# A decoder layer's attention: when norm factors and operand splits are computed, and how rotary scores are multiplied

## The chip, the core and the metric

One Trainium2 chip, of which the kernel uses one core. A core has TensorE (PE, matrix products; PEld its weight loads), VectorE (DVE), ScalarE (ACT), GpSimd (POOL) and SyncE (SP, which here issues most transfers), and they run side by side, held together by semaphores only. The metric is the device time of one execution in microseconds. The kernel before takes 1430.42 us, the median of three runs (1427.04 to 1432.64).

## The reference

A decoder layer over 1024 tokens of width 1024: adaLN-modulated RMS norm, one input projection, eight heads of stick-breaking attention (width 64) and four heads of softmax attention (MLA), an output projection, and a SwiGLU FFN. What the change touches is this:

```
q = rms_norm(q, q_norm); k_nope = rms_norm(k_nope, ...); k_rope = rms_norm(k_rope, ...)
q = concat([q[..., :128], apply_rope(q[..., 128:], positions)])          # 4 heads, 128 + 64 wide
k = concat([k_nope, broadcast(apply_rope(k_rope, positions), 4 heads)])  # one rotary key for all heads
o_mla = causal_softmax_attention(q, k, v_mla)                            # scores of 192 products each
mixed = concat([rms_norm(o_sb, out_norm_sb), rms_norm(o_mla, out_norm_mla)])
x = x + gate1 * (mixed @ w_out)
```

## The kernel before, in words

Matrix products are taken in a rounded fp32 type. To keep fp32 precision each operand x is split into a high part H (ScalarE's rounding copy) and a low part L = x - H (VectorE's subtraction), and a product is the sum of three: H.H + H.L + L.H (`three`, L1579). A *split* here is such a pair of instructions on a [128, 1024] tile; they count semaphores m_h and m_l.

The softmax attention runs in 32 units: two pairs of heads p (0, 1), two heads e in each, eight query blocks of 128 in each head, in the order ORDER0, so that the units of a head have 1, 7, 3, 5, 6, 4, 8 and 2 key blocks. v is the unit's number in its pair (0 to 15), u = 16 p + v. The sequence positions are reversed, hence the causal part lies to the right. TensorE's order is written out by hand (L1921): in turn n it issues `scores(n+2)`, `turned(n)` (transposes of the weights, 128 columns each) and `values(n-1)`. `scores` takes segments of up to 512 columns: three products for the 128 plain rows, three for the rotary rows (`mla_scores`, L1764), and a mask on the first segment. The rotary rows of both heads of a pair lie in one tile QRK[:, p] (64 rows each), and the head is picked by the key's tile: KRH[e] and KRL[e] have the rotary key in 64 rows and zeros, written by GpSimd, in the other 64.

VectorE, per unit (`mla_step`, L1260): maximum of the scores, its negation, its share of the copy of the turned weights of u-2, the finish of u-3. ScalarE, per unit (L790): exponential with row sum, its share of that copy (pmT). Both then do splits: at v = 2 q and k of the pair's second head; at v = 12 rotary part, q and k of the next pair's first head (p = 0), or q and k of the first stick-breaking pair (p = 1). `mla_ready` (L1833) makes TensorE wait for the counts of m_l.

The stick-breaking attention has 64 units, in four pairs of heads (i = 0 to 3), 16 units each, numbered v. ScalarE makes two sigmoids, omb and beta, VectorE a scan (left) and a product, then come turns and values as above. Its scores take two products for a segment and not three: the high part and the low part of a head's 64 rows of q are stacked in one 128-row tile headQ, against the key's high part twice, headKH, and its low part with zeros, headKL. SP builds these tiles by five transfers for each head (`stack_head`, L388).

In the last pair ScalarE also makes the norm of the softmax outputs: the squares' sums of o_mla for eight token blocks at v = 0 to 7 (`mla_squares`), VectorE the mean at v = 9, GpSimd the power -0.5 (nrs), and ScalarE scales the blocks at v = 10 to 13, two in each, after waiting for nrs at v = 10. Each of these stands at the head of ScalarE's step, ahead of omb. The blocks are then transposed, rounded and multiplied by w_out, whose first two splits stand at v = 11 and 12.

Of the kernel before, what the change touches and what calls it, by code (L numbers as in the profile page):

```python
# [23 lines left out]
P = 128  # L24
# [80 lines left out]

SPLIT1, SPLIT0 = 2, 12
SB_Q, SB_K, SB_OUT = 4, 6, 11
# [12 lines left out]
def build(nc, xT, cols_d, rows_d, pos_d, ada1_d, ada2_d, win_d, qup_d, kvup_d, wout_d, gu_d, down_d, x2_d, t_d, out_d):  # L120
# [82 lines left out]
    pmT = [at(f"pmT{s}", [P, S], F32, 18 + 4 * s) for s in range(2)]  # L203
    KRH = [at("KRH0", [P, S], F32R, 26), at("KRH1", [P, S], F32R, 98)]
    KRL = [at("KRL0", [P, S], F32R, 30), at("KRL1", [P, S], F32R, 102)]
# [4 lines left out]

    mrH = [at("mrH0", [P, S], F32R, 138), at("mrH1", [P, S], F32R, 142)]
    mrL = [at("mrL0", [P, S], F32R, 202), at("mrL1", [P, S], F32R, 158)]
# [77 lines left out]
    t_out = [ctx.enter_context(nc.semaphore(f"t_out{k}")) for k in range(2)]  # L290
    traw_in = [ctx.enter_context(nc.semaphore(f"traw_in{k}")) for k in range(2)]
    head_in = [ctx.enter_context(nc.semaphore(f"head_in{e}")) for e in range(2)]
    raw_in = [ctx.enter_context(nc.semaphore(f"raw_in{k}")) for k in range(2)]
# [3 lines left out]
    def after(n):  # L297

        return n + 1 + PRIME
# [56 lines left out]
    def _(sp):  # L356
# [31 lines left out]
        def stack_head(p, e):  # L388

            own, other = slice(64 * e, 64 * e + 64), slice(64 - 64 * e, 128 - 64 * e)  # L390
            sp.wait_ge(sem["s_h"], 2 * p + 2)
            sp.wait_ge(sem["s_l"], 2 * p + 2)
            for dst, src in ((headQ[e][own, :], pairQH[own, :]), (headQ[e][other, :], pairQL[own, :]), (headKH[e][own, :], pairKH[own, :]),
                             (headKH[e][other, :], pairKH[own, :]), (headKL[e][own, :], pairKL[own, :])):
                sp.dma_start(dst.bitcast(F32), src.bitcast(F32)).then_inc(head_in[e], 16)

        stack_head(0, 0)
# [77 lines left out]
    def _(pool):  # L475
# [52 lines left out]
        for e in range(2):  # L528
            o = 64 * (1 - e)
            pool.memset(KRH[e][o:o + 64, :].bitcast(F32), 0.0).then_inc(sem["kr_zero"], 1)  # L530
            pool.memset(KRL[e][o:o + 64, :].bitcast(F32), 0.0).then_inc(sem["kr_zero"], 1)
# [36 lines left out]
    def _(act):  # L568
# [135 lines left out]

        def mla_split(p, e, t=slice(0, S)):

            if p or e:
                act.wait_ge(sem["m_qk"], PRIME if p == 0 else after(NU * (p - 1) + (7 if e == 0 else NU - 1)))
            if e == 0:
                A(mrH[p][:, t], QRK[:, p, t], ACT.Copy).then_inc(sem["m_h"], 1)  # L710
            A(mqH[e][:, t], QN[:, 2 * p + e, t], ACT.Copy).then_inc(sem["m_h"], 1)
            A(mkH[e][:, t], KN[:, 2 * p + e, t], ACT.Copy).then_inc(sem["m_h"], 1)

# [5 lines left out]
        act.wait_ge(sem["t_dve"], after(NT - 2))  # L719
        mla_split(0, 0, slice(0, S - P))  # L720
        turn_out(NT - 1)
        act.wait_ge(sem["t_act"], 2 * NT + PRIME)
        act.wait_ge(sem["t_dve"], after(NT - 1))
        act.sem_inc(sem["low_over"], 1)
        mla_split(0, 0, slice(S - P, S))


        for e in range(2):
            o = 64 * e
            A(KRH[e][o:o + 64, :], QRK[o:o + 64, 2, :], ACT.Copy).then_inc(sem["kr_h"], 1)  # L730
            values_out(4 + 2 * e)

# [57 lines left out]
        def mla_step(u):  # L790

            p, v = divmod(u, NU)
            n = BLOCKS[v] * P
            act.wait_ge(sem["m_nm"], after(u))
            act.wait_ge(sem["m_tr"], after(u - 2))
            A(pm[v % 2][:, 0:n], pair(2 * (v % 2), n), ACT.Exp, bias=nmx[:, v:v + 1], scale=QK ** -0.5,
              accum_out=den[:, v:v + 1]).then_inc(sem["m_exp"], 1)
            if u >= 2:
                mla_copy(u - 2, (u - 2) % NU)
            if v == SPLIT1:  # L800
                mla_split(p, 1)
            if v == SPLIT0:
                if p == 0:
                    mla_split(1, 0)
                else:
                    stick_q(0)
                    stick_k(0)

        def stick_step(u):
# [4 lines left out]
            if last and SB_OUT <= v < SB_OUT + 2:  # L814
                split(H_OUT + v - SB_OUT, H_OUT + v - SB_OUT, 0)
            if last and v < NT:
                if v:
                    act.wait_ge(sem["n_sq"], v)
                mla_squares(v)
            if last and v == NT + 2:  # L820
                act.wait_ge(sem["n_r"], 1)
            if last and NT + 2 <= v < NT + 6:
                for k in range(2):
                    mla_scale((4 + 2 * (v - NT - 2) + k) % NT)
            if u == 0:
# [155 lines left out]
    def _(dve):  # L981
# [226 lines left out]

        def mla_split(p, e, t=slice(0, S), done=3):

            ops = [(mqL[e], QN[:, 2 * p + e, t], mqH[e]), (mkL[e], KN[:, 2 * p + e, t], mkH[e])]
            if e == 0:
                ops = [(mrL[p], QRK[:, p, t], mrH[p])] + ops
            for k, (lo, x, hi) in enumerate(ops):
                dve.wait_ge(sem["m_h"], done + 5 * p + 3 * e + k + 1)
                V.tensor_tensor(lo[:, t], x, hi[:, t], ALU.subtract).then_inc(sem["m_l"], 1)

        values_out(1)
        values_out(3)
        mla_split(0, 0, slice(0, S - P), 0)  # L1220
        turn_out(NT - 1)
        mla_split(0, 0, slice(S - P, S))


        dve.wait_ge(sem["low_over"], 1)
        for e in range(2):
            o = 64 * e
            dve.wait_ge(sem["kr_h"], e + 1)
            V.tensor_tensor(KRL[e][o:o + 64, :], QRK[o:o + 64, 2, :], KRH[e][o:o + 64, :], ALU.subtract).then_inc(sem["kr_l"], 1)
            values_out(5 + 2 * e)  # L1230
# [29 lines left out]
        def mla_step(u):  # L1260
# [9 lines left out]
            if u >= 3:  # L1270
                mla_finish(u - 3)
            if v == SPLIT1:
                mla_split(p, 1)
            if v == SPLIT0:
                if p == 0:
                    mla_split(1, 0)
                else:
                    stick_q(0)
                    stick_k(0)

# [13 lines left out]
        def stick_step(u):  # L1294
# [20 lines left out]
            if last and SB_OUT <= v < SB_OUT + 2:  # L1315
                wsplit(H_OUT + v - SB_OUT, H_OUT + v - SB_OUT)
            if last and v == NT + 1:
                dve.wait_ge(sem["n_sq"], NT)
                V.tensor_scalar(nms[:], nss[:], 1.0 / 512, EPS, ALU.mult, ALU.add).then_inc(sem["n_ms"], 1)
# [254 lines left out]
    def _(pe):  # L1574
# [189 lines left out]
        def mla_scores(p, e, q0, out, k0, w, diagonal):  # L1764
            q, k = slice(q0, q0 + P), slice(k0, k0 + w)
            three(out, mqH[e][:, q], mqL[e][:, q], mkH[e][:, k], mkL[e][:, k], True, False)
            last = three(out, mrH[p][:, q], mrL[p][:, q], KRH[e][:, k], KRL[e][:, k], False, not diagonal)
            if diagonal:
# [64 lines left out]
        def mla_ready(u):  # L1833

            p, v = divmod(u, NU)
            if v == 0:
                pe.wait_ge(sem["m_l"], 6 + 5 * p)
            elif v == NU // 2:
                pe.wait_ge(sem["m_l"], 8 + 5 * p)
            if u == NU // 2:  # L1840
                pe.wait_ge(sem["kr_zero"], 4)
                pe.wait_ge(sem["kr_l"], 2)
# [71 lines left out]
        pe.wait_ge(sem["vt_odd"], 2)  # L1914
        pe.wait_ge(sem["kr_zero"], 2)
        pe.wait_ge(sem["kr_l"], 1)
# [222 lines left out]
```

## Time and profile before

| | us |
|---|---|
| median of three runs | 1430.42 |
| the profiled execution's own time | 1429.01 |
| its span | 1427.2 |
| busy: PE / PEld / DVE / ACT / POOL | 1327.7 / 1102.4 / 812.1 / 556.1 / 64.5 |
| mean granted TensorE clock, as a share of full speed | 0.977 |

The span is the time from the first to the last instruction of the profiled execution. All instants below are counted from its start. The softmax part lies at 341 to 450, the stick-breaking part at 452 to 631. A row of the timeline gives start, duration, engine, line, operation, out<-in and, in brackets, the engine's idle time before it and what released it. "Granted clock" 1.00 is 2.4 GHz, 0.50 is 1.2 GHz.

### The profile page before, as it was taken

The numbers are of one execution on the slowest core, as the hardware profiler recorded it, in microseconds if no ns is written. First come the engines' busy times: TensorE is split into PE (matmuls) and PEld (weight loads), VectorE is DVE, ScalarE is ACT, GpSimd is POOL, SyncE is SP. The second block draws the span as 40 slices with busy tenths as digits, with TensorE's granted clock in tenths as the row PEclk, the third lists the DMA queues.
The fourth block names the chain that finished last, engine by engine and source line by source line (L and its number), as shares of the span: only waits on it lengthen the run. The fifth ranks groups of instructions, "written<-read, shape, count | busy, mean of one in ns | idle before, by whom it ended". The sixth has DMA issues, their size and how long they took to land.

```text
span 1427.2 us, 17303 instructions
## 1 busy us (share of the span) xinstructions
PE 1327.7 (93%) x6696; PEld 1102.4 (77%) x6696; DVE 812.1 (57%) x1183; ACT 556.1 (39%) x904; POOL 64.5 (5%) x70
## 2 busy tenths in 40 slices
PE   3999999787998889988989999999999989999998
PEld 2688878676887778877867788888888877887886
DVE  6543454577556887954368666556666642335333
ACT  4512212456435776882145333333333322322231
POOL 1001000231000000010000000000000000001001
PEclk9999999999999998999999999999999999999999
DMA  9242433000003322510140311222222125446443
GB/s 381 81 195 103 174 113 112 1 0 1 1 1 75 75 51 61 186 30 30 44 167 40 118 65 70 89 89 89 89 89 85 64 82 198 141 151 237 164 141 125
DMA packets 37261, 142.96 MB, mean 100 GB/s; under 512 B 4160, under 2 KB 4288, under 8 KB 35648
## 3 DMA queue, kind: packets, MB, share of 16 engines
q1 hardware_dynamic: 34848, 133.51, 27.7%
q0 software_dynamic: 2336, 8.39, 1.6%
q8 instruction: 52, 0.85, 0.3%
q14 instruction: 25, 0.20, 0.0%
HBM read 111.48 MB, written 19.92 MB: 92 GB/s over the span
## 4 chain that ended last, share of the span: by engine, by line
PE 73%; DVE 13%; issue 6%; ACT 4%; DMA 2%; POOL 2%; DVEq 0%; SPq 0%; ACTq 0%; POOLq 0%
PE ps L2039 26%; PE ps L1592 15%; PE ps L1581 8%; PE ps L1583 8%; PE ps L1582 8%; DVE left L1301 4%; PE ps L1807 2%; PE ps L1829 1%; PE ps L1796 1%; POOL rstd L522 1%; DVE beta L1306 1%; PE ps L1816 1%; PE ps L1625 1%; ACT omb L829 1%; DMA t_spill_d<-tst 1%
## 5 line engine op out<-in xcount | busy, mean ns | idle before, releaser
L1581 PE MATMUL ps<-TH,dWH 128*128 128x512 f32 x352 | 137.9, 392 | 6.7 <-DVE dWL L1549 5.8
L1582 PE MATMUL ps<-TL,dWH 128*128 128x512 f32 x352 | 137.7, 391 | 0.0
L1583 PE MATMUL ps<-TH,dWL 128*128 128x512 f32 x352 | 137.5, 391 | 0.0
L2039 PE MATMUL ps<-h2H,slH 128*128 128x512 f32 x320 | 125.0, 391 | 2.3 <-ACT s L951 2.3
L2039 PE MATMUL ps<-h2L,slH 128*128 128x512 f32 x320 | 125.0, 391 | 0.0
L2039 PE MATMUL ps<-h2H,slL 128*128 128x512 f32 x320 | 125.0, 391 | 0.0
L1547 DVE TENSOR_TENSOR TL<-traw,TH 128x512 fp32r<-128x512 f32 x44 | 30.5, 693 | 138.0 <-ACT TH L972 138.0
L934 ACT ACTIVATE slH<-ssum 128x512 fp32r<-128x512 f32 x80 | 50.4, 632 | 146.2 <-PE ps L2039 96.4
L1301 DVE TENSOR_TENSOR_SCAN left<-omb 128x1023 f32<-128x1023 f32 (+6 forms) x64 | 86.3, 1349 | 20.6 <-ACT omb L829 20.6
L972 ACT ACTIVATE TH<-traw 128x512 fp32r<-128x512 f32 x44 | 27.8, 631 | 168.4 <-PE ps L1583 150.7
L1581 PEld LDWEIGHTS ps<-TH,dWH 128*128 128x128 f32 x352 | 66.4, 189 | 21.9 <-issue 6.6
L1024 DVE TENSOR_TENSOR WL<-raw,WH 128x1024 fp32r<-128x1024 f32 x30 | 38.4, 1280 | 74.3 <-ACT WH L578 74.3
L1592 PE MATMUL ps<-hH,WH 128*128 128x512 f32 x256 | 79.7, 392 | 0.8 <-DVE WL L1024 0.8
L1592 PE MATMUL ps<-hL,WH 128*128 128x512 f32 x256 | 78.9, 389 | 0.0
L1592 PE MATMUL ps<-hH,WL 128*128 128x512 f32 x256 | 78.8, 389 | 0.0
L1583 PEld LDWEIGHTS ps<-TH,dWL 128*128 128x128 f32 x352 | 66.5, 189 | 13.8
L1582 PEld LDWEIGHTS ps<-TL,dWH 128*128 128x128 f32 x352 | 66.4, 189 | 13.7
L1829 PE MATMUL ps<-VS,wT 128*128 128x64 f32 x576 | 76.5, 281 | 0.0
L1829 PEld LDWEIGHTS ps<-VS,wT 128*128 128x128 f32 x576 | 74.7, 204 | 0.2
L2039 PEld LDWEIGHTS ps<-h2H,slH 128*128 128x128 f32 x320 | 60.2, 188 | 15.2 <-DVE slL L1494 2.7
L2039 PEld LDWEIGHTS ps<-h2H,slL 128*128 128x128 f32 x320 | 60.4, 189 | 12.5
L2039 PEld LDWEIGHTS ps<-h2L,slH 128*128 128x128 f32 x320 | 60.3, 188 | 12.5
(315 smaller groups left out, 2972.9 us busy)
## 6 DMA issues: line engine op xcount, KB each, us to landing
ada<-ada SPq DMA_DIRECT2D x12, 2048.0 KB, 8.1
draw<-down SPq DMA_DIRECT2D x44, 512.0 KB, 3.6
sraw<-gu SPq DMA_DIRECT2D x20, 1024.0 KB, 5.9
traw<-t_spill_d SPq DMA_DIRECT2D x44, 256.0 KB, 3.9
t_spill_d<-tst SPq DMA_DIRECT2D x20, 512.0 KB, 3.0
raw<-win SPq DMA_DIRECT2D x18, 512.0 KB, 3.6
x_in<-xT SPq DMA_DIRECT2D x4, 1024.0 KB, 8.7
headKH<-pairKH SPq DMA_DIRECT2D x16, 256.0 KB, 4.7
```

Of the source, the lines that this page charges most:

```text
L934: A(slH[q][:], operand(u, q), ACT.Copy).then_inc(sem["g_h"], 1)
L972: A(TH[d % 2][:], traw[d % 2][:], ACT.Copy).then_inc(sem["th_done"], 1)
L1024: V.tensor_tensor(WL[par % 2][:], raw[r % 2][:], WH[par % 2][:], ALU.subtract).then_inc(sem["split_l"], 1)
L1301: V.tensor_tensor_scan(left[v % 2][:, 1:n], omb[v % 2][:, 0:n - 1], omb[v % 2][:, 0:n - 1], 1.0, ALU.mult, ALU.bypass).then_inc(sem["s_sca ...
L1547: V.tensor_tensor(TL[d % 2][:], traw[d % 2][:], TH[d % 2][:], ALU.subtract).then_inc(sem["tl_done"], 1)
L1581: mm(out, lh, rh, start=first, stop=False)
L1582: mm(out, lh, rl, start=False, stop=False)
L1583: return mm(out, ll, rh, start=False, stop=last)
L1592: last = mm(ps[:, b + hf, :], l[s][:, j * P:(j + 1) * P], cut(r, j, half(hf)), start=(j == 0 and k == 0), stop=(j == KD - 1 and k == 2))
L1807: last = mm(ps[:, 6 + v % 2, 0:VD], pmT[v % 2][:, k * P:(k + 1) * P], VM[:, qt + k, (2 * i + e) * VD:(2 * i + e + 1) * VD], start=(k == 0) ...
L1829: last = mm(ps[:, bank, c:c + SBD], wT[v % 2][:, k * P:(k + 1) * P], VS[:, qt + k, (2 * i + e) * SBD:(2 * i + e + 1) * SBD], start=(k == 0 ...
L2039: last = mm(ps[:, Q_BANK[q], :], l[q][:, w], r[:, c, :], start=(c == 0 and k == 0 and q not in (Q_G2, Q_S4)), stop=(c == 3 and k == 2), sk ...
```

## The change

Three edits in one.

- **Rotary scores.** For each head a tile headR[p][e] holds the high part of the head's 64 rotary query rows in its own rows and the low part in the other 64, brought there by a transfer of SP from mrL (four transfers of 64 rows by 4 KB, semaphores rope_in). KRH is one tile with the rotary key in both halves. A segment takes headR.KRH and headR.KRL[e]. Only the first two units keep three products, on 64 rows. The rotary rows are split per head (64 rows) and not per pair.
- **Splits one by one.** At (p, v) of SPLIT_AT, one split each.
- **Norm factors.** Squares and mean move to the third pair (v = 0 to 7 and v = 10), ScalarE waits for the factors at v = 0 of the last pair, and scales one block in each of its units 0 to 7.

Changed lines, each group with the line before it:

```diff
@@ -103,7 +103,9 @@
 NG1 = G1_BEFORE[NU]
-SPLIT1, SPLIT0 = 2, 12
+SPLIT_AT = {(0, 1): ("q", 0, 1), (0, 3): ("k", 0, 1), (0, 9): ("r", 1, 0), (0, 10): ("q", 1, 0), (0, 12): ("k", 1, 0), (0, 14): ("r", 1, 1),
+            (1, 1): ("q", 1, 1), (1, 3): ("k", 1, 1), (1, 10): ("stick q", 0, 0), (1, 12): ("stick k", 0, 0)}
+SPLIT_ORDER = [("r", 0, 0), ("q", 0, 0), ("k", 0, 0)] * 2 + [("r", 0, 1)] + list(SPLIT_AT.values())
@@ -201,14 +203,14 @@
     pmT = [at(f"pmT{s}", [P, S], F32, 18 + 4 * s) for s in range(2)]
-    KRH = [at("KRH0", [P, S], F32R, 26), at("KRH1", [P, S], F32R, 98)]
+    KRH = at("KRH", [P, S], F32R, 98)
     mkL = [at(f"mkL{e}", [P, S], F32R, 118 + 16 * e) for e in range(2)]
-    mrH = [at("mrH0", [P, S], F32R, 138), at("mrH1", [P, S], F32R, 142)]
+    headR = [[at("headR00", [P, S], F32R, 138), at("headR01", [P, S], F32R, 26)], [at("headR10", [P, S], F32R, 142), at("headR11", [P, S], F32R, 146)]]
@@ -289,6 +291,7 @@
     traw_in = [ctx.enter_context(nc.semaphore(f"traw_in{k}")) for k in range(2)]
+    rope_in = [ctx.enter_context(nc.semaphore(f"rope_in{e}")) for e in range(4)]
@@ -393,6 +396,12 @@
                 sp.dma_start(dst.bitcast(F32), src.bitcast(F32)).then_inc(head_in[e], 16)
+        for p in range(MH // 2):
+            for e in range(2):
+                own, other = slice(64 * e, 64 * e + 64), slice(64 - 64 * e, 128 - 64 * e)
+                sp.wait_ge(sem["m_l"], max(4, SPLIT_ORDER.index(("r", p, e)) + 1))
+                sp.dma_start(headR[p][e][other, :].bitcast(F32), mrL[p][own, :].bitcast(F32)).then_inc(rope_in[2 * p + e], 16)
@@ -527,7 +536,6 @@
             o = 64 * (1 - e)
-            pool.memset(KRH[e][o:o + 64, :].bitcast(F32), 0.0).then_inc(sem["kr_zero"], 1)
@@ -702,14 +710,27 @@
             A(VS[:, tt, :], ps[:, tt, :], ACT.Copy).then_inc(sem["vt_even"], 1)
-        def mla_split(p, e, t=slice(0, S)):
-            if p or e:
-                act.wait_ge(sem["m_qk"], PRIME if p == 0 else after(NU * (p - 1) + (7 if e == 0 else NU - 1)))
-            if e == 0:
-                A(mrH[p][:, t], QRK[:, p, t], ACT.Copy).then_inc(sem["m_h"], 1)
-            A(mqH[e][:, t], QN[:, 2 * p + e, t], ACT.Copy).then_inc(sem["m_h"], 1)
-            A(mkH[e][:, t], KN[:, 2 * p + e, t], ACT.Copy).then_inc(sem["m_h"], 1)
+        def mla_split(what, p, e, t=slice(0, S)):
+            if p and (what, e) != ("r", 1):
+                act.wait_ge(sem["m_qk"], after(NU * (p - 1) + (7 if e == 0 else NU - 1)))
+            own = slice(64 * e, 64 * e + 64) if what == "r" else slice(0, P)
+            dst, src = {"r": (headR[p][e], QRK[:, p, :]), "q": (mqH[e], QN[:, 2 * p + e, :]), "k": (mkH[e], KN[:, 2 * p + e, :])}[what]
+            A(dst[own, t], src[own, t], ACT.Copy).then_inc(sem["m_h"], 1)
+        def first_split(t):
+            for what in "rqk":
+                mla_split(what, 0, 0, t)
+        def next_split(what, p, e):
+            if what == "stick q":
+                stick_q(p)
+            elif what == "stick k":
+                stick_k(p)
+            else:
+                mla_split(what, p, e)
@@ -717,18 +738,18 @@
         act.wait_ge(sem["t_dve"], after(NT - 2))
-        mla_split(0, 0, slice(0, S - P))
+        first_split(slice(0, S - P))
         act.sem_inc(sem["low_over"], 1)
-        mla_split(0, 0, slice(S - P, S))
-        for e in range(2):
-            o = 64 * e
-            A(KRH[e][o:o + 64, :], QRK[o:o + 64, 2, :], ACT.Copy).then_inc(sem["kr_h"], 1)
-            values_out(4 + 2 * e)
+        first_split(slice(S - P, S))
+        A(KRH[:], QRK[:, 2, :], ACT.Copy).then_inc(sem["kr_h"], 1)
+        values_out(4)
+        mla_split("r", 0, 1)
+        values_out(6)
@@ -797,14 +818,8 @@
                 mla_copy(u - 2, (u - 2) % NU)
-            if v == SPLIT1:
-                mla_split(p, 1)
-            if v == SPLIT0:
-                if p == 0:
-                    mla_split(1, 0)
-                else:
-                    stick_q(0)
-                    stick_k(0)
+            if (p, v) in SPLIT_AT:
+                next_split(*SPLIT_AT[p, v])
@@ -813,15 +828,14 @@
                 split(H_OUT + v - SB_OUT, H_OUT + v - SB_OUT, 0)
-            if last and v < NT:
+            if i == SBH // 2 - 2 and v < NT:
                 mla_squares(v)
-            if last and v == NT + 2:
+            if last and v == 0:
                 act.wait_ge(sem["n_r"], 1)
-            if last and NT + 2 <= v < NT + 6:
-                for k in range(2):
-                    mla_scale((4 + 2 * (v - NT - 2) + k) % NT)
+            if last and v < NT:
+                mla_scale((4 + v) % NT)
@@ -1206,27 +1220,41 @@
             V.tensor_copy(VS[:, tt, :], ps[:, tt, :]).then_inc(sem["vt_odd"], 1)
-        def mla_split(p, e, t=slice(0, S), done=3):
-            ops = [(mqL[e], QN[:, 2 * p + e, t], mqH[e]), (mkL[e], KN[:, 2 * p + e, t], mkH[e])]
-            if e == 0:
-                ops = [(mrL[p], QRK[:, p, t], mrH[p])] + ops
-            for k, (lo, x, hi) in enumerate(ops):
-                dve.wait_ge(sem["m_h"], done + 5 * p + 3 * e + k + 1)
-                V.tensor_tensor(lo[:, t], x, hi[:, t], ALU.subtract).then_inc(sem["m_l"], 1)
+        def mla_split(what, p, e, k, t=slice(0, S)):
+            dve.wait_ge(sem["m_h"], k + 1)
+            own = slice(64 * e, 64 * e + 64) if what == "r" else slice(0, P)
+            lo, x, hi = {"r": (mrL[p], QRK[:, p, :], headR[p][e]), "q": (mqL[e], QN[:, 2 * p + e, :], mqH[e]), "k": (mkL[e], KN[:, 2 * p + e, :], mkH[e])}[what]
+            V.tensor_tensor(lo[own, t], x[own, t], hi[own, t], ALU.subtract).then_inc(sem["m_l"], 1)
+        def first_split(k, t):
+            for n, what in enumerate("rqk"):
+                mla_split(what, 0, 0, k + n, t)
+        def next_split(what, p, e):
+            if what == "stick q":
+                stick_q(p)
+            elif what == "stick k":
+                stick_k(p)
+            else:
+                mla_split(what, p, e, SPLIT_ORDER.index((what, p, e)))
         values_out(3)
-        mla_split(0, 0, slice(0, S - P), 0)
+        first_split(0, slice(0, S - P))
         turn_out(NT - 1)
-        mla_split(0, 0, slice(S - P, S))
+        first_split(3, slice(S - P, S))
             o = 64 * e
-            dve.wait_ge(sem["kr_h"], e + 1)
-            V.tensor_tensor(KRL[e][o:o + 64, :], QRK[o:o + 64, 2, :], KRH[e][o:o + 64, :], ALU.subtract).then_inc(sem["kr_l"], 1)
+            dve.wait_ge(sem["kr_h"], 1)
+            V.tensor_tensor(KRL[e][o:o + 64, :], QRK[o:o + 64, 2, :], KRH[o:o + 64, :], ALU.subtract).then_inc(sem["kr_l"], 1)
+            if e:
+                mla_split("r", 0, 1, 6)
@@ -1269,14 +1297,8 @@
                 mla_finish(u - 3)
-            if v == SPLIT1:
-                mla_split(p, 1)
-            if v == SPLIT0:
-                if p == 0:
-                    mla_split(1, 0)
-                else:
-                    stick_q(0)
-                    stick_k(0)
+            if (p, v) in SPLIT_AT:
+                next_split(*SPLIT_AT[p, v])
@@ -1314,7 +1336,7 @@
                 wsplit(H_OUT + v - SB_OUT, H_OUT + v - SB_OUT)
-            if last and v == NT + 1:
+            if i == SBH // 2 - 2 and v == NT + 2:
@@ -1764,7 +1786,11 @@
             three(out, mqH[e][:, q], mqL[e][:, q], mkH[e][:, k], mkL[e][:, k], True, False)
-            last = three(out, mrH[p][:, q], mrL[p][:, q], KRH[e][:, k], KRL[e][:, k], False, not diagonal)
+            if (p, e) == (0, 0) and q0 // P in ORDER0[:2]:
+                last = three(out, headR[0][0][0:64, q], mrL[0][0:64, q], KRH[0:64, k], KRL[0][0:64, k], False, not diagonal)
+            else:
+                mm(out, headR[p][e][:, q], KRH[:, k], start=False, stop=False)
+                last = mm(out, headR[p][e][:, q], KRL[e][:, k], start=False, stop=not diagonal)
@@ -1834,11 +1860,17 @@
             if v == 0:
-                pe.wait_ge(sem["m_l"], 6 + 5 * p)
+                pe.wait_ge(sem["m_l"], SPLIT_ORDER.index(("k", 1, 0)) + 1 if p else 6)
+                if p:
+                    pe.wait_ge(rope_in[2], 16)
             elif v == NU // 2:
-                pe.wait_ge(sem["m_l"], 8 + 5 * p)
+                pe.wait_ge(sem["m_l"], SPLIT_ORDER.index(("k", p, 1)) + 1)
+                pe.wait_ge(rope_in[2 * p + 1], 16)
+            if u == 2:
+                pe.wait_ge(rope_in[0], 16)
+                pe.wait_ge(sem["kr_zero"], 1)
             if u == NU // 2:
-                pe.wait_ge(sem["kr_zero"], 4)
+                pe.wait_ge(sem["kr_zero"], 2)
@@ -1912,7 +1944,6 @@
         pe.wait_ge(sem["vt_odd"], 2)
-        pe.wait_ge(sem["kr_zero"], 2)
```

## Rows read from the trace of the kernel before

**Rows 1.** Busy microseconds of each engine in the softmax part, then granted clock, DMA share, GB/s.

```profile
341.40:449.60 108.20, 101.37 (x716) 88.74 (x714) 65.21 (x158) 46.71 (x105) 2.46 (x5) 1.00 0.06 12
```

**Rows 2.** Groups of instructions in the softmax part: count, busy, mean ns, idle before.

```profile
L1265 DVE TENSOR_REDUCE mx<-ps 128x1 f32<-128x128 f32 (+7 forms) x32 | 24.2, 755 | 22.2 <-PE ps L1583 17.2 <-PE ps L1769 4.4
L796 ACT ACTIVATE pm<-ps,nmx 128x128 f32<-128x128 f32 (+7 forms) x32 | 23.7, 741 | 61.0 <-DVE nmx L1267 50.8 <-PE ps L1796 10.3
L738 ACT ACTIVATE pmT<-ps 128x256 f32<-128x256 f32 (+3 forms) x30 | 12.8, 428 | 0.0
```

**Rows 3.** Timeline (start, duration, engine, line) at the softmax unit with eight blocks.

```profile
361.66 1.23 DVE L1265 TENSOR_REDUCE mx<-ps 128x1 f32<-128x1024 f32 x1 [2.36 <-PE ps L1583]
364.79 0.41 PE L1796 MATMUL ps<-ident,pm 128*128 128x128 f32 x2 [0.62 <-ACT pm L796]
```

**Rows 4.** TensorE's timeline at rotary products; last, mrL's instructions in the softmax part.

```profile
341.79 0.28 PE L1581 MATMUL ps<-KRH,mrH 128*128 128x128 f32 x1
341.90 0.28 PE L1582 MATMUL ps<-KRL,mrH 128*128 128x128 f32 x1
...
348.29 0.39 PE L1581 MATMUL ps<-KRH,mrH 128*128 128x512 f32 x1
348.52 0.40 PE L1582 MATMUL ps<-KRL,mrH 128*128 128x512 f32 x1
...
341.40:449.60 108.20, 16.64 (x48) 9.06 (x48) 1.22 (x1) 1.00 0.06 12
```

**Rows 5.** Timeline at softmax unit 12 (three splits) and the turns behind it.

```profile
383.21 1.06 ACT L710 ACTIVATE mrH<-QRK 128x1024 fp32r<-128x1024 f32 x1
...
384.30 1.22 DVE L1216 TENSOR_TENSOR mrL<-QRK,mrH 128x1024 fp32r<-128x1024 f32 x1 [0.99 <-ACT mrH L710]
...
387.71 0.68 DVE L1265 TENSOR_REDUCE mx<-ps 128x1 f32<-128x512 f32 x1
...
389.88 0.85 PE L1796 MATMUL ps<-ident,pm 128*128 128x128 f32 x6 [1.56 <-ACT pmT L738]
```

**Rows 6.** TensorE's waits in the softmax part: total us, times, longest.

```profile
PE ps L1796 <- ACT pmT L738: 3.9, 3, 1.6
```

**Rows 7.** VectorE's timeline at the first maximum.

```profile
343.59 0.28 DVE L1265 TENSOR_REDUCE mx<-ps 128x1 f32<-128x128 f32 x1
```

**Rows 8.** Timeline of SP's head transfers and TensorE's first stick-breaking score.

```profile
442.85 0.54 SPq L395 DMA_DIRECT2D headQ<-pairQH  x1
446.03 1.23 SPq L395 DMA_DIRECT2D headKL<-pairKL  x1
...
452.05 0.30 PE L1774 MATMUL ps<-headKH,headQ 128*128 128x128 f32 x1 [2.48 <-issue]
```

**Rows 9.** Timeline in the last pair's unit 10, and its last unit's scores.

```profile
605.22 0.39 PE L1775 MATMUL ps<-headKL,headQ 128*128 128x512 f32 x1
...
606.85 1.64 POOL L543 TENSOR_TENSOR nrs<-nms,nhalf 128x8 f32<-128x8 f32 x1 [157.99 <-DVE nms L1319]
...
609.76 1.00 ACT L829 ACTIVATE omb<-ps 128x1024 f32<-128x1024 f32 x1
...
611.71 1.30 PE L1816 MATMUL ps<-ident,beta 128*128 128x128 f32 x5 [4.06 <-ACT wT L746]
...
625.69 0.30 PE L1774 MATMUL ps<-headKH,headQ 128*128 128x128 f32 x1
```

**Rows 10.** One wait of TensorE, and two stretches with their granted clock.

```profile
555.78 1.39 PE L1816 MATMUL ps<-ident,beta 128*128 128x128 f32 x8 [1.29 <-DVE beta L1306]
...
560.00:570.00 10.00, 10.00 (x44) 8.84 (x43) 6.45 (x6) 4.50 (x8) 0.00 (x0) 0.50 0.47 97
610.00:620.00 10.00, 8.19 (x43) 7.40 (x43) 8.36 (x8) 10.00 (x14) 0.00 (x0) 0.66 0.00 0
```

**Rows 11.** Timeline of the third pair's unit 6: its omb and its scan.

```profile
549.29 1.02 ACT L829 ACTIVATE omb<-ps 128x1024 f32<-128x1024 f32 x1 [0.18 <-PE ps L1775]
...
552.11 2.28 DVE L1301 TENSOR_TENSOR_SCAN left<-omb 128x1023 f32<-128x1023 f32 x1
```

## The prediction

> **What bounds the kernel now.** I read the page first: busy time by engine, the slices, the chain that ended last. The change touches only the attention, so I then asked for windows of that stretch, for TensorE's waits in it, and for the timeline around each of these waits. In the softmax part (341.4 to 449.6) TensorE is busy 101.4 of 108.2 us, VectorE 65 and ScalarE 47 [rows 1]: TensorE bounds it, and what it lacks is a handful of waits. In the stick-breaking part behind it VectorE's scans share the path. From 631 on the output projection runs on TensorE without a gap that this change touches, so that a time saved before it moves the end by itself.
>
> How the softmax part is coupled: the turns of unit u-1 wait until ScalarE has copied the turned weights of unit u-2, and ScalarE does that only after the exponential of unit u, which needs VectorE's maximum of u. This chain (maximum 0.76, negation and handover 0.2, exponential 0.74, copy 0.43, handovers 0.3: 2.4 us on average [rows 2]) runs beside TensorE's own work of a unit, which is 101.4/32 = 3.1 to 3.2 us (idle are 6.8 by [rows 1], and 7.5 if the gaps in the timeline are added up one by one). So TensorE has 0.7 us to spare on average. It is not even: at the unit with eight blocks the chain from 361.66 ends at 364.79 and TensorE has waited 0.62 [rows 3].
>
> **Part 1: one rotary product less.** A head's score segments are, by columns, six of 512 and two each of 384, 256 and 128: 12, times four heads = 48 [rows 4]. Start to start a 512-column product takes 0.23 us and one of 128 columns 0.11 [rows 4]; for 384 and 256 I take 0.18 and 0.12, between these. A head saves 6 x 0.23 + 2 x (0.18 + 0.12 + 0.11) = 2.20, four heads 8.8; the first two units keep three products (0.11 + 0.23 + 0.18), which leaves **8.3 us of TensorE work saved**. The stacked operand has 128 rows, as the zero-padded one had, so a product costs what it did.
> The Trainium skill (TensorE: Matmul & The Clock Gate, "Back-to-back issue gap") gives about 131 ns per 512-column matmul in a stream of weight loads and matmuls. By that the saving would be some 5 us. The trace disagrees: 0.23 us apart.
> That work is only on the path while TensorE has no wait. Taking 0.26 us per unit from it leaves a spare of 0.5 on average. By the sizes of the blocks I get, from v = 1 to 8 of each head: 0.2, 0.55, 0.2, 0.4, 1.3, -0.9, 0.55, 1.75.
>
> **Part 2: splits spread.** Before, three splits sit in one unit (12) and pairs at units 2, 18, 28. At unit 12 ScalarE's highs start at 383.21, VectorE's first low at 384.30 and the others every 1.14 us, the third ends at 387.80; only then comes the next maximum (387.71), and the turns start at 389.88 with TensorE waiting 1.56 [rows 5]. In all, waits for the copy cost 3.9 us in three places [rows 6]. From the same rows, one split alone ends 2.2 us after the copy before it (1.0 high, 1.2 low), which makes the next maximum 1.9 late, less the spare of its own unit; what the next unit cannot spare either is a new wait. A pair costs 1.14 more, three cost 2.28 more. This rule gives 1.8 for unit 12 (seen: 1.56, and 0.38 just behind it), so I trust it. Single splits now follow units 1, 3, 9, 10, 12, 14, 17, 19, 26, 28, mostly where the spare is smallest:
> - units 1 and 3: VectorE has one more low (1.2 us) in front of its last value copy, and the first maximum, 343.59 [rows 7], comes at 344.8; then the split of unit 1 stands in front of the maximum of unit 2, which before ran at once. Waits about 1.25 (there before), 2.1, 1.25, and 0.9 at unit 6: 5.5 us, where the timeline has 2.9 now.
> - unit 9: 1.9 - 0.2 - 0.55 = 1.2. Unit 10, straight behind: no spare is left, 1.8. Unit 12: absorbed by the 1.3 of its neighbour. Unit 14: 0.9 for the eight blocks, and 1.9 - 0.55 = 1.4.
> - unit 17: 1.2; unit 19: 0.8 (the wait before has given it some spare); unit 22: 0.9.
> - unit 26: 1.2; unit 28: none; unit 30: 0.9.
> Sum 15.8 against the 7.5 that stand now: **+8.3 us of waits**. That eats the saved product; TensorE gets to its first stick-breaking score at about the same time, by the unit-by-unit count 0.8 earlier. The bounds: if all new waits are hidden, the part gains 8.3 + 5 of the present waits; if the half of mine that comes from neighbouring splits is twice as large, it loses 3.
> What follows gains: the first stick-breaking score waits 2.48 for the stacked heads, whose first transfer is issued at 442.85, when the pair of unit 28 is through, and whose last is issued at 446.03 [rows 8]. With its q half done two units earlier the transfers start 2.4 earlier against unit 26 (one high and one low), and this wait falls from 2.5 to about 0.8. **Softmax part with its handover: -2.5 us.**
>
> **Part 3: rotary transfers, zeroing, first scores.** Four more transfers of 256 KB on SP's queue, ahead of the head stacks. The first is issued when the second slice of mrL is there (338.8) and must land before unit 2's scores (344.8 before, about 345.7 now): like transfers land in 3 to 5 us, so it is in time by 2. The other three have over 10 us, and SP is idle until 442.85, so nothing behind them waits. A late one would cost its lateness once, 0 to 2 us. Two of four memsets on GpSimd go; the first score waited for KRL, not for them: nothing. **0.**
>
> **Part 4: norm factors in the third pair.** At unit 10 of the last pair ScalarE stands still until GpSimd's factors, begun at 606.85, are there at 608.5, then scales twice, and only at 609.76 starts omb; the scores of this unit had ended at 605.6 [rows 9]. TensorE waits 4.06 for the copy queued behind this, restarts at 611.71 and runs at a mean granted clock of 0.66 in the ten microseconds from 610 [rows 9, 10], so for most of them at the lower of its two levels, 1.2 and 2.4 GHz: five turns take 1.30 there. With factors and scales done earlier, omb of unit 10 starts at 605.65 instead of 609.76. Followed through, ScalarE (no scales of 1.35 in units 10 to 13, but omb, copy, beta and the w_out splits) then sets turns of units 10 and 11 a microsecond late each, and the scores of the last unit come at 620.25, not 625.69: **-5.4 us**, 4.1 of it the wait and 1.3 the slow clock. Bounds: 4.1 to 6.5 (the second if the two late turns are hidden).
> What it costs: eight squares move to units 0 to 7 of the third pair. Each takes 0.61 from start to the next instruction, beside the q and k splits. There VectorE runs without a gap and ScalarE is ahead: at unit 6, behind the q split, omb is done at 550.3 and its scan starts at 552.11 [rows 11]. Three squares use up this 1.8: 0 to 1 us lost, I take 0.3. In the last pair eight scales stand where eight squares of the same length stood: 0.
>
> **The sum**: -2.5 - 5.4 + 0.3 = -7.6 on the profiled execution's 1429.0: 1421.4. The median of the runs is 1.4 above that execution, so **1422.8**.
>
> **Rivals.**
> 1. The spread splits are hidden better than by my rule, because a wait at one unit gives spare to the next two. For it: the pair of unit 28 shows only 0.43 of wait. Against: the rule met unit 12. Half of my 15.8 goes: another -7, 1415.8.
> 2. The clock. TensorE's granted clock was 0.50 from 560 to 570, behind a wait of 1.29 at 555.78 and smaller ones before it [rows 10]. In the softmax part, which TensorE bounds, fifteen such microseconds would cost about 7. My new waits at units 1 to 3 and 9 to 11 are of that kind; the longer ones of before (1.56 and 0.38) did not bring it down. One fall: 1429.8. **Falls at both places, lasting half as long again as that one, add 14 and end at 1437, slower than before**; it decides from the second fall on.
> The Trainium skill ("The HAM clock gate" of the same page) has it that idleness throttles the array and sustained work releases it. By that rule more and longer waits make this rival likelier, and the 4.06 us wait that goes gives clock back; the trace's 0.66 behind that wait agrees.
> 3. The factors move but the end does not follow, because ScalarE stays the bound in the last eight units: only the clock comes back. Then -2.5 - 1.3 + 0.3: 1426.9. For it: ScalarE is busy all of 610 to 620. Against: 5.4 us of this are scales that leave.
>
> **Chances.** Forecast 0.50, rival 1 0.20, one clock fall 0.10, both 0.08, rival 3 0.12. The 80% range: 1412 to 1431, which takes in rivals 1 and 3 and one fall and the run-to-run spread of 5.6 us. Half a per cent is 7.2 us, about what a measurement of this kernel can tell, so the lines are 1423.3 and 1437.6, the first right at the forecast: 0.3 of its 0.5 lies below, 0.2 more with rival 1 and 0.02 for the spread of the others: faster 0.52. Slower 0.06, most of the two falls; the rest, 0.42, the same.
>
> **What would show it.** The 144 rotary products (3 x 48) become 99: two for each segment, three for the three segments of the first two units. Of TensorE's waits for pmT, more and shorter ones than the three of [rows 6], at units 1, 3, 10, 11, 15, 17; GpSimd's factors near 560 and no wait of 4 us in the last pair; clock 1.0 there; the first stick-breaking score with under 1 us of wait. Waits in the softmax part under 8 us in sum would prove part 2 wrong, a first-pair clock under 0.9 would be rival 2, and an omb of the last pair's unit 10 that still waits over 2 us would be rival 3.

## The result, and the profile after

The changed kernel takes 1420.59 us (median of 17 runs, 1415.56 to 1429.30), the kernel before, on the same chips, 1429.63 us (17 runs). The ratio is 0.9946, with a 95% interval of 0.9929 to 0.9964: 7.7 us less by the ratio, which is the figure with an interval, and 9.0 by the medians.

The profiled execution is not a typical one: 1428.12 us at a mean granted clock of 0.976. The 17 runs fall in two groups: eleven with a clock of 0.981 to 0.984 took 1415.6 to 1422.1, six with 0.975 to 0.978 took 1425.5 to 1429.3. So the span of one execution doesn't tell what the change is worth here, and I compare stretches of the profiled executions instead. "Softmax part" is the time from the first softmax score to the first stick-breaking score, "rest" from there to the product with w_out's first part before which TensorE waits 4.34 us in every one of these kernels. "Waits" are the times in which TensorE is idle for over 0.15 us in the softmax part, the wait for the stacked heads at its end included.

| kernel | softmax part | waits in it | rest | ratio of runs (95%) |
|---|---|---|---|---|
| before | 110.6 | 9.3 | 210.4 | 1 |
| changed | 109.0 | 14.2 | 207.4 | 0.9946 (0.9929 to 0.9964) |
| e1 norm factors alone | 110.9 | 9.3 | 199.3 | 0.9958 (0.9942 to 0.9974) |
| e2 rotary edit alone | 111.4 | 11.4 | 215.2 | 1.0014 (1.0000 to 1.0028) |
| e3 changed, splits in lumps | 111.7 | 13.0 | 201.8 | 0.9958 (0.9943 to 0.9973) |
| e4 low one unit later | 100.5 | 6.8 | 200.1 | 0.9880 (0.9852 to 0.9908) |
| e5 third product again | 112.8 | 9.5 | 200.2 | 0.9961 (0.9947 to 0.9975) |
| e6 changed, norm as before | 109.1 | 14.2 | 206.7 | 0.9993 (0.9980 to 1.0005) |
| e7 before, low one unit later | 110.6 | 8.9 | 213.7 | 1.0019 (1.0003 to 1.0034) |
| e8 e4, heads earlier | 97.8 | 4.2 | 205.0 | 0.9864 (0.9840 to 0.9888) |
| e9 changed, copy first | 100.4 | 6.5 | 200.1 | 0.9885 (0.9863 to 0.9907) |
| e10 e8 and copy first | 93.6 | 1.2 | 201.7 | 0.9818 (0.9794 to 0.9843) |

(What the rest contains: one or two falls of TensorE's granted clock where it is 199 to 202 us; two or three, or the 4 us wait of the last pair, where it is 205 to 210; five where it is 214 or 215. So it differs from execution to execution by more than most of the edits are worth.)

Windows of the changed kernel, to be set against [rows 1, 10]. Each line gives the stretch, its length, the busy us of PE, PEld, DVE, ACT and POOL with their counts, the granted clock, the DMA share and GB/s:

```profile
342.00:450.60 108.60, 94.80 (x672) 81.90 (x670) 67.10 (x160) 47.90 (x106) 2.03 (x4) 1.00 0.10 22
520.00:530.00 10.00, 10.00 (x45) 8.73 (x44) 6.45 (x6) 4.96 (x9) 0.00 (x0) 0.52 0.41 87
612.00:622.00 10.00, 9.24 (x80) 8.55 (x79) 9.69 (x14) 7.95 (x14) 0.00 (x0) 1.00 0.24 64
```

TensorE is busy 94.8 us in the softmax part, where it was 101.4, in a part that is hardly shorter. Around 616, in the last pair, the granted clock is 1.00 now, where [rows 10] have 0.66. It falls elsewhere instead: 0.52 from 520 to 530 (1.00 before), 0.66 from 470 to 480 (1.00 before) and still 0.66 from 560 to 570. So this execution, with a mean granted clock of 0.976, is hardly faster than the one profiled before, with 0.977. The rotary products on 128 rows are two groups of 45, where three groups of 48 were before. Those of 512 columns start 0.23 us apart, as in [rows 4]:

```profile
L1792 PE MATMUL ps<-KRH,headR 128*128 128x512 f32 (+3 forms) x45 | 15.7, 348 | 0.0
L1793 PE MATMUL ps<-KRL,headR 128*128 128x512 f32 (+3 forms) x45 | 15.5, 344 | 0.0
```

```profile
349.58 0.39 PE L1792 MATMUL ps<-KRH,headR 128*128 128x512 f32 x1
349.81 0.40 PE L1793 MATMUL ps<-KRL,headR 128*128 128x512 f32 x1
```

TensorE's waits (total, times, longest) for the exponential and for the copy, against [rows 6], and the first of them in the timeline:

```profile
PE ps L1822 <- ACT pm L817: 7.8, 8, 1.7
PE ps L1822 <- ACT pmT L759: 4.8, 4, 1.5
```

```profile
352.56 0.52 PE L1822 MATMUL ps<-ident,pm 128*128 128x128 f32 x3 [1.72 <-ACT pm L817]
359.65 0.74 PE L1822 MATMUL ps<-ident,pm 128*128 128x128 f32 x5 [0.91 <-ACT pm L817]
...
366.67 0.63 PE L1822 MATMUL ps<-ident,pm 128*128 128x128 f32 x4 [0.73 <-ACT pm L817]
379.58 0.96 PE L1822 MATMUL ps<-ident,pm 128*128 128x128 f32 x7 [1.11 <-ACT pm L817]
384.11 0.52 PE L1822 MATMUL ps<-ident,pm 128*128 128x128 f32 x3 [1.49 <-ACT pmT L759]
...
394.25 0.63 PE L1822 MATMUL ps<-ident,pm 128*128 128x128 f32 x4 [0.74 <-ACT pm L817]
398.10 1.06 PE L1822 MATMUL ps<-ident,pm 128*128 128x128 f32 x8 [1.31 <-ACT pmT L759]
```

They stand where the prediction's rule for single splits put them: behind the splits of units 1 and 3 (1.72, 0.91), at the eight-block unit (0.73), behind units 9 and 10 (1.11, 1.49), at the eight-block unit and behind unit 14 (0.74, 1.31). The profile calls some of them "<-ACT pm", the exponential. But the exponential of the unit that is turned was long done then; the instruction waits for the copy pmT too, and TensorE starts 0.1 us after that copy ends (352.46 and 352.56).

The stacked heads' transfers and the first stick-breaking score, against [rows 8]: a wait of 0.43 where it was 2.48.

```profile
442.68 0.46 SPq L398 DMA_DIRECT2D headQ<-pairQH  x1
...
445.79 1.21 SPq L398 DMA_DIRECT2D headKL<-pairKL  x1
...
451.05 0.30 PE L1800 MATMUL ps<-headKH,headQ 128*128 128x128 f32 x1 [0.43 <-issue]
```

The norm factors and the end of the last pair, against [rows 9]: the factors are begun at 572, unit 10 starts its omb as soon as its scores are there, and there is no wait of 4 us. The largest wait that is left in this pair is 0.50.

```profile
572.28 2.67 POOL L551 TENSOR_TENSOR nrs<-nms,nhalf 128x8 f32<-128x8 f32 x1 [123.10 <-DVE nms L1341]
...
608.13 1.02 ACT L843 ACTIVATE omb<-ps 128x1024 f32<-128x1024 f32 x1 [1.44 <-PE ps L1801]
...
613.26 1.06 PE L1842 MATMUL ps<-ident,beta 128*128 128x128 f32 x8 [0.31 <-ACT wT L767]
...
621.70 0.30 PE L1800 MATMUL ps<-headKH,headQ 128*128 128x128 f32 x1
```

### The profile page after: what moved, and what is told of

It is laid out like the page before. It is cut to its first block, busy times and chain, and to the rows that moved or that the text cites. A ratio compares the mean times of both kernels' runs of the same rounds, so it can differ in the third digit from the quotient of the medians.

```text
span 1426.3 us, 17219 instructions
## 1 busy us (share of the span) xinstructions
PE 1322.3 (93%) x6651; PEld 1097.5 (77%) x6651; DVE 813.7 (57%) x1185; ACT 556.9 (39%) x905; POOL 63.8 (4%) x68
## 4 chain that ended last, share of the span: by engine, by line
PE 74%; DVE 12%; issue 5%; ACT 5%; DMA 2%; POOL 2%; DVEq 0%; SPq 0%; ACTq 0%; POOLq 0%
PE ps L2070 26%; PE ps L1614 15%; PE ps L1603 8%; PE ps L1605 7%; PE ps L1604 7%; DVE left L1323 3%; PE ps L1855 2%; PE ps L1842 1%; PE ps L1833 1%; DVE mx L1293 1%; POOL rstd L531 1%; PE ps L1822 1%; DVE beta L1328 1%; ACT omb L843 1%; PE ps L1800 1%
```

## The experiments

Ten kernels, each against the kernel before on the same chip. e1 to e4 ran together, e5 to e8, and e9 with e10.

### The parts alone: e1, e2, e3, e6

e1 is the third edit, the norm factors, alone on the kernel before. e6 is the changed kernel with that edit taken back. e3 is the changed kernel with the splits in lumps (shortened; a loop over each list goes with it):

```diff
-SPLIT_AT = {(0, 1): ("q", 0, 1), (0, 3): ("k", 0, 1), (0, 9): ("r", 1, 0), ...
+SPLIT_AT = {(0, 2): [("q", 0, 1), ("k", 0, 1)], (0, 12): [("r", 1, 0), ("q", 1, 0), ("k", 1, 0)],
+            (1, 2): [("r", 1, 1), ("q", 1, 1), ("k", 1, 1)], (1, 12): [("stick q", 0, 0), ("stick k", 0, 0)]}
```

e2 is e3 with the norm edit taken back.

> The kernel before with part 4 alone: squares and mean in the third pair, scales in units 0 to 7 of the last. My theory: the 4.1 us wait at unit 10 of the last pair goes, with some of the slow clock behind it, 0.3 us come back in the third pair: 5.1 us faster than before (ratio 0.9964). The softmax part (first softmax score to first stick-breaking score, 110.6 us) unchanged within 0.3. Rival (ScalarE stays the bound of the last eight units): 2 us faster or less. Rival (all of the measured 9 us comes from this edit): 8 to 9 us faster.

> The changed kernel with the norm factors back in the last pair: rotary edit and spread splits alone. My theory: softmax part 109.0 as in the changed kernel (before 110.6), the 4.1 us wait of the last pair is back: 1.6 us faster than before (0.9989). If the three edits add up, e1 (0.9958) and this give the changed kernel's 0.9946. Rival (the spread splits calm the clock all over the attention, too): 3 us or more faster than before.

e1: 0.9958, 6.0 us. e6: 0.9993, 1.0 us, the softmax part 109.1. 0.9958 x 0.9993 = 0.9951, the changed kernel has 0.9946: within the intervals the edits add up. e1's interval, 3.7 to 8.3 us, excludes its first rival. It only just touches the second (8 to 9 us), which the last pair below and e6 speak against. The rival of e6 (3 us or more) falls outside its interval. The wait of the last pair is back in e6:

```profile
604.98 1.30 PE L1843 MATMUL ps<-ident,beta 128*128 128x128 f32 x5 [4.08 <-ACT wT L767]
```

From the scan of its unit 8 to the transposes of o_mla the last pair takes 23.8 us before and 24.1 in e6, and 17.3 in the changed kernel, e1 and e3: 6.5 less, where the prediction had 5.4 and 6.5 as its bound. In the third pair, with no fall of the clock in either, the first half (scan of unit 0 to that of unit 8), in which the squares stand, takes 21.8 us in e1 and in e6; the second half, in which VectorE's mean stands, takes 18.6 in e1 and 18.4 in e6. So the move costs 0.2.

> The changed kernel with the norm factors put back where they were and the splits in lumps as before (three at unit 12, pairs at 2 and 28; the second rotary half of pair 1 joins the pair of unit 18). So the rotary edit alone. My theory of waits: work 8.3 us less, waits about 12.4 instead of 7.5, stacked heads 1.1 later than in the changed kernel: the softmax part 5 us shorter than before, the whole 5.3 us faster (0.9963). Rival (TensorE alone bounds it, lumps cost what they cost before): 8.3 us faster or more. Rival (splits in lumps were the reason for spreading them, the shorter work only lengthens the waits): within 2 us of before.

> The changed kernel with the splits in lumps again. My theory: spreading them costs, since each single one stands in front of VectorE's next maximum; waits 12.4 us in four or five places instead of 14.3 in fourteen, softmax part 2.8 us shorter than in the changed kernel, the whole 10.4 us faster than before (0.9927). Rival (spreading is what makes the product's saving count): 2 to 5 us slower than the changed kernel.

Both missed: the softmax part, forecast 5 us shorter in e2 and 2.8 us shorter than the changed kernel's in e3, became longer in both. The second rival of e2 (within 2 us of before) has the time that was measured, 2.0 us slower. With the product gone and the splits in lumps, the softmax part takes 111.4 and 111.7 us, longer than with both as before. The waits are about those of the prediction's rule. A lump of three delays the next maximum by 1.9 + 2.28; less the prediction's spares of the two units concerned (0.4 + 1.3, and 0.55 + 0.2), that makes 2.5 behind unit 12 (2.2 seen) and 3.4 behind unit 18 (3.6 seen):

```profile
387.20 0.85 PE L1824 MATMUL ps<-ident,pm 128*128 128x128 f32 x6 [2.23 <-ACT pmT L759]
...
409.47 0.87 PE L1824 MATMUL ps<-ident,pm 128*128 128x128 f32 x3 [3.56 <-ACT pmT L759]
```

What the expectation left out is the clock. The same window of e3 and, below it, of e1, whose lumps leave waits of 1.56 (at 389.31) and 1.51 (at 409.50):

```profile
410.00:420.00 10.00, 10.00 (x53) 8.52 (x52) 3.21 (x9) 2.43 (x6) 0.00 (x0) 0.72 0.00 0
```

```profile
410.00:420.00 10.00, 9.71 (x69) 8.34 (x67) 5.04 (x14) 3.78 (x9) 0.22 (x1) 1.00 0.01 2
```

In e3 the granted clock is below 1 in all four ten-us windows from 380 to 420 (0.91, 0.92, 0.93, 0.72; e2: 0.95, 0.88, 0.98, 0.68), in e1, before and the changed kernel it is 1.00 there. The shares missing in e3's four windows add up to 5.2 us of full-speed time, and e3's part came 5.4 later than expected against the changed kernel (2.6 longer instead of 2.8 shorter). So in these executions spreading the splits paid through the clock and not through waits. That rests on one profiled execution of each kernel. In the whole time e3 and the changed kernel can't be told apart (their intervals overlap); the same step without the norm edit, e2 against e6, is 1.0014 against 0.9993, which points the same way but overlaps as well. With the splits in lumps the saved product brought nothing: e3 and e1 both have 0.9958. e2 is 1.4 in a thousand slower than before, more than its softmax part explains; its profiled execution has five falls of the clock in the stick-breaking part, and why it has more of them than others stays open.

### What the product is worth: e5

```diff
                 mm(out, headR[p][e][:, q], KRH[:, k], start=False, stop=False)
+                mm(out, headR[p][e][:, q], KRL[e][:, k], start=False, stop=False)
                 last = mm(out, headR[p][e][:, q], KRL[e][:, k], start=False, stop=not diagonal)
```

> The changed kernel with one product more in each rotary segment from unit 2 on (headR.KRL a second time, so the scores are not the layer's), all else as it is: the price of the product in this schedule. 45 segments, 8.3 us of TensorE work. By my rule the spare of each unit rises by 0.26 and the new waits shrink from 14.8 to about 11: softmax part 4.5 us longer than the changed kernel's 109.0, the whole 4.5 us slower than it (0.9978 of before). Rival (TensorE bounds and the waits stay): 8.3 longer. Rival (the saved product only turned into waits): under 2 longer.

The softmax part became 3.8 longer, where 4.5 was expected, and its waits 9.5 instead of 14.2. So 8.3 us of TensorE work are worth 3.8 us of this part, and the rest turns into waits, as the prediction's first two steps have it; both rivals, 8.3 and under 2, fall. The whole is 0.0015 x 1429 = 2.1 us slower than the changed kernel, but there the intervals overlap, so the 3.8 rests on the two profiled executions.

### Which wait it is: e4, e7, e8, e9, e10

e4, on VectorE only:

```diff
-            if (p, v) in SPLIT_AT:
-                next_split(*SPLIT_AT[p, v])
+            if divmod(u - 1, NU) in SPLIT_AT:
+                next_split(*SPLIT_AT[divmod(u - 1, NU)])
```

> The changed kernel, but VectorE makes each low one unit after ScalarE's high, behind its maximum, negation, copy and finish. If the new waits are there because VectorE stands still for ScalarE's high in front of its next maximum (my theory), most of them go: about 7 us of waits left (startup and the three units of eight blocks), the first stick-breaking score earlier by 5 us though its heads are stacked one unit later; 5 us faster than the changed kernel. Rival (VectorE's 1.2 us for the low itself is what is late, wherever it stands): 1 us or less.

Softmax part 109.0 to 100.5, the whole 1429 x (0.9946 - 0.9880) = 9.4 us faster than the changed kernel, more than the 5 that were expected, with the same instructions in the same places of TensorE and ScalarE. The waits that are left in that part are those at the four eight-block units, the one for the heads and one near the start:

```profile
PE ps L1822 <- ACT pm L817: 3.0, 4, 0.7
PE ps L1800 <- issue: 2.6, 1, 2.6
PE ps L1603 <- ACT pm L817: 1.2, 1, 1.2
```

The low of 1.2 us still stands ahead of a maximum in e4; only the standing still for ScalarE's high is gone, and with it every wait behind a split. So that standing still, and not the low itself, was the cost of a spread split.

> The kernel before, its splits in lumps as they are, but VectorE makes its lows one unit after ScalarE's highs. If waits come from VectorE standing still for the highs, the waits of 0.8, 1.56, 0.38 and 1.52 at units 2, 12, 18 go (4 us); the stacked heads come 1.9 us later: softmax part 2 us shorter than before's 110.6, the whole 0.9985. Rival (what e4 gained comes from spreading and the later low together): no change.

The same edit as e4's, on the kernel before, whose splits stay in lumps. A miss: the part is as long as before's and the whole 2.7 us slower (0.0019). The waits behind the pairs of units 2 and 18 go, but the three lows of unit 13, in one lump, still delay a maximum (1.58 left), and the wait for the heads grows from 2.48 to 4.17:

```profile
452.92 0.44 PE L1774 MATMUL ps<-headKH,headQ 128*128 128x128 f32 x1 [4.17 <-issue]
```

The rival's outcome is the one that was measured: on the lumps the later low brings nothing. The other waits did shrink, from 6.8 to 4.7; the heads took 1.7 of that back, and from 450 to 460 the granted clock is 0.66, where the kernel before has 1.00. Lumps with a later low and earlier heads were not tried.

> e4 (low one unit later) with the stick-breaking pair's q and k split at units 24 and 26, not 26 and 28. In e4 TensorE waits 2.60 us for the stacked heads. If nothing else holds the first stick-breaking score, that wait falls under 0.3 and the softmax part from 100.5 to 98.2: 2.3 us faster than e4, 0.9865 of before. Rival: the two splits now stand at units with less spare and bring waits of their own, 1 us or less gained.

`(1, 10)` and `(1, 12)` of the stick-breaking pair became `(1, 8)` and `(1, 10)`. The wait for the heads is gone, the softmax part 97.8 (2.7 shorter, expected 2.3). In the whole it is 0.9864 against 0.9880: the expected size, but the intervals overlap.

e9 and e10, on ScalarE in `mla_step` (shortened):

```diff
+            if u >= 2:
+                mla_copy(u - 2, (u - 2) % NU)
             act.wait_ge(sem["m_nm"], after(u))
             ...
             A(pm[v % 2][:, 0:n], pair(2 * (v % 2), n), ACT.Exp, ...
-            if u >= 2:
-                mla_copy(u - 2, (u - 2) % NU)
```

> The changed kernel, but ScalarE copies the turned weights of unit u-2 before the exponential of unit u, not after it. My rule has every wait of the softmax part come from this chain (maximum, exponential, copy, then the turns of u-1). If so, the three waits of 0.74 at the units with eight blocks go and those behind splits shrink: the turns then wait for an exponential that is a unit old. Waits 14.8 down to about 5, softmax part from 109.0 to 99 to 101, the whole 8 to 10 us faster than the changed kernel. Rival (the next scores, which wait for the exponential, take the waits over): 2 us or less, since the exponential itself comes no earlier.

> e8 (low one unit later, stick-breaking splits at units 24 and 26) with the copy ahead of the exponential as well. The remaining 4 waits of 0.74 at eight-block units go: softmax part from 97.8 to 95; the whole 2.5 to 3 us faster than e8 (0.9864), about 0.9845. Rival (as in e9): no change against e8.

e9: part 100.4, the whole 8.7 us faster than the changed kernel, as expected. ScalarE's copy is waited for nowhere any more; what remains is VectorE's half of it, behind splits, the heads and two waits near the start:

```profile
PE ps L1822 <- DVE pmT L1265: 2.9, 2, 1.6
PE ps L1800 <- issue: 1.8, 1, 1.8
PE ps L1603 <- ACT pm L819: 1.7, 2, 1.2
```

e10: part 93.6, 0.9818 of before, 26 us. It is the fastest, 18 us faster than the changed kernel, and gained more over e8 than expected: 4.2 us in the part instead of 2.8, and 6.6 in the whole instead of 2.5 to 3 (the intervals of e8 and e10 just overlap). Two waits are left in that part, 1.2 us in sum, both near its start and neither at an exponential's transposes (L1822):

```profile
PE ps L1603 <- ACT pm L819: 0.9, 1, 0.9
PE ps L1603 <- issue: 0.3, 1, 0.3
```

## Why the prediction was right, point by point

- **The whole**: 1422.8 was forecast, a change of -7.6; 1420.59 and -7.7 were measured. That the sum came so close is luck: its two main terms were off by one us each, in opposite directions, and the interval of the measured change is 5.1 to 10.1 us.
- **Part 1, the product**: right. 45 segments with two products, start to start as before. e5 shows that the 8.3 us of work are real and that 3.8 of them reach the time.
- **Part 2, the new waits**: right in mechanism, and too high in size. 15.8 us were forecast, 13.8 were there, at the units named. The waits that stood before were 6.8 and not the 7.5 that the prediction took, and there was no wait of 0.38 behind unit 12: its rule gave 1.8 there where 1.56 was seen, so it was already a little too high. So the waits grew by 7.0, not by 8.3, and the wait for the heads fell by 2.05, to 0.43, where 1.7 less was forecast.
- **The term of the softmax part** came out as -1.6 by the profile and -1.0 by e6's runs, not -2.5. What the sum left out is that TensorE's time outside its waits fell by less than the product's 8.3 us: part less waits is 101.3 before and 94.8 now, 6.5 less. The table shows one reason. The same products take, part less waits, 92.4 us in e10, with two waits, 93.7 in e4, with six, and 94.8 in the changed kernel, with fifteen. By these a wait costs some 0.15 to 0.2 us beyond its gap, an estimate, or about 1.3 for the seven waits more than before. Part of what then remains is at the change of rows that the last section shows.
- **Part 3**: right. The transfer for unit 2 was issued at 339.43 and landed 2.9 us later, well ahead of unit 2's scores, which start at 346.56, just behind the end of the first exponential (346.3). The first maximum is 3.4 us behind the first score, where it was 2.2 [rows 7], as the prediction had it from VectorE's additional low.
- **Part 4**: right in mechanism, mis-sized by one: -6.5 in the last pair instead of -5.4. The two late turns for which the prediction allowed one us each are waits of 0.31 and 0.44. The move costs 0.2 in the third pair, not 0.3. The factors were begun at 572 and not near 560, which changed nothing, since the last pair starts at 584.
- **Rival 1** (waits hidden better) did not happen, but e4 and e9 reach what it was worth.
- **Rival 2, the clock**: not in this schedule's softmax part. Its granted clock stays at 1.00 there, with waits up to 1.72. It did happen in e2 and e3, in windows with waits of 2.2 and 3.6. The Trainium skill (TensorE: Matmul & The Clock Gate, "The HAM clock gate") says that idleness throttles the array. The trace agrees where it has 0.72 around and behind the 3.6 us wait. But the length of a wait alone doesn't tell: behind the 2.59 us wait for the heads in e4 the clock stays at 1.00, and in e2 it is 0.50 from 348.2 to 351.4, right behind a wait of 1.15. What decides is not shown.

```profile
440.00:450.00 10.00, 8.96 (x68) 7.60 (x69) 6.90 (x14) 6.68 (x12) 0.00 (x0) 1.00 0.53 117
```

- **Rival 3**: excluded by e1, and omb of unit 10 waits for nothing but its scores.
- **The chances**: 0.52 for a gain of half a per cent or more stood on a median right at that line. The measured 0.9946 lies just beyond it (0.9950), and its interval holds it.

## What to carry to other kernels

Work taken from the busiest engine is worth only what its waits leave of it: count the spare of each step, not the busy share. Where two engines share a task (one makes a high part, the other subtracts), let the second take its part one step later; spreading alone puts its standing still in front of the critical chain once per piece. Copy what is ready before waiting for what is not: the order of two instructions on ScalarE, which is busy less than half of this part, was worth 8.7 us. Count the waits too, since each seems to cost a little more than its gap, and look at the granted clock before comparing two spans.

## What the hardware showed beside

The first two units take their rotary products on 64 rows, the others on 128. Where the row count changes, the next product starts late in this trace. TensorE's timeline of the changed kernel, first unit:

```profile
342.16 0.27 PE L1604 MATMUL ps<-mkL,mqH 128*128 128x128 f32 x1
342.27 0.27 PE L1605 MATMUL ps<-mkH,mqL 128*128 128x128 f32 x1
342.47 0.32 PE L1603 MATMUL ps<-KRH,headR 64*128 64x128 f32 x1
342.64 0.27 PE L1604 MATMUL ps<-KRL,headR 64*128 64x128 f32 x1
```

128-column products stand 0.11 us apart, but 0.20 from the last one with 128 rows (342.27) to the first with 64 (342.47), and 0.17 to the next. In the second unit's segment of 512 columns it is 0.32 and 0.34 instead of 0.23 (starts at 343.31, 343.54, 343.86, 344.20). No experiment separates this from the change of the weights' tile, which alone costs nothing between 128-row products (0.11 from 342.16 to 342.27).
